# Seams of a two-layer diffusion step: the first two chunks' high parts made by ScalarE straight from the transposes

## The reference: what is computed

```python
def layer(x, mod, p, ...):
    sh1, sc1, g1, sh2, sc2, g2 = jnp.split(mod, N_MOD, axis=-1)
    h = rms_norm(x, p["g_pre_mix"]) * (1.0 + sc1) + sh1
    y, ckv, krope, hf, hb = mixer(h, p, ...)      # projections, attention, RG-LRU, w_out
    x = x + g1 * rms_norm(y, p["g_post_mix"])
    h = rms_norm(x, p["g_pre_ffn"]) * (1.0 + sc2) + sh2
    x = x + g2 * rms_norm(swiglu(h, p), p["g_post_ffn"])
    return x, ckv, krope, hf, hb
```

## Time and profile before

| | before |
|---|---|
| device time, median of 3 runs (lowest to highest) | 1274.1 us (1274.09 to 1274.28) |
| span of the profiled execution | 1276.9 us |
| PE busy | 1239.6 us, 97% |
| PEld, DVE, ACT busy | 1145.4, 853.3, 658.0 us |
| POOL busy | 19.6 us |
| the three seams, time of tile 0's last root | 375.9, 664.3, 992.4 us |

### The profile page before, as it was taken

How to read it: one execution, slowest core, us unless ns; L and a number is a source line. 1 busy time by engine, 2 the same in 40 slices (tenths; PEclk the granted TensorE clock), 3 DMA queues, 4 the chain that set the end, 5 groups by cost and what they waited for, 6 DMA issues and landing times.

```text
span 1276.9 us, 19343 instructions
## 1 busy us (share of the span) xinstructions
PE 1239.6 (97%) x7345; PEld 1145.4 (90%) x7345; DVE 853.3 (67%) x1391; ACT 658.0 (52%) x1161; POOL 19.6 (2%) x41
## 2 busy tenths in 40 slices
PE   6999999999999999999999999999999999999998
PEld 4899989978879999998879999998898899999886
DVE  2697684764869888868858885856566748433423
ACT  5479874754464333332255999647446533333322
POOL 0000000200000000000000000011000000000000
PEclk9999999999989999999999999999999999999999
DMA  9645555332437776758815333442224347444441
GB/s 336 211 116 178 182 165 197 103 120 100 124 117 221 255 224 203 235 178 272 286 49 144 110 100 115 128 140 75 76 80 152 107 146 231 132 132 132 158 165 49
DMA packets 131103, 199.33 MB, mean 156 GB/s; under 512 B 10330, under 2 KB 70980, under 8 KB 131012
## 3 DMA queue, kind: packets, MB, share of 16 engines
q1 hardware_dynamic: 131012, 198.11, 48.8%
HBM read 196.16 MB, written 1.92 MB: 155 GB/s over the span
## 4 chain that ended last, share of the span: by engine, by line
PE 77%; DVE 11%; ACT 6%; issue 2%; DMA 2%; SPq 1%; DVEq 0%; ACTq 0%
PE bank L755 16%; PE bank L762 16%; PE bank L763 16%; PE bank L885 5%; PE bank L887 5%; PE bank L886 5%; DVE weight_low L1700 3%; ACT weight_high L1318 2%; PE bank L1185 1%; DVE lru_h L1998 1%; PE bank L1209 1%; ACT sq L1326 1%; DVE lru_tau L2002 1%; DVE lru_i L1994 1%; PE bank L1194 1%
## 5 line engine op out<-in xcount | busy, mean ns | idle before, releaser
L762 PE MATMUL bank<-act_low,weight_high 128*128 128x384 f32 x1440 | 488.5, 339 | 3.7 <-DVE weight_low L1700 3.6
L763 PE MATMUL bank<-act_high,weight_low 128*128 128x384 f32 x1440 | 483.4, 336 | 0.0
L1700 DVE TENSOR_TENSOR weight_low<-raw,weight_high 128x1024 fp32r<-128x1024 f32 (+5 forms) x282 | 320.2, 1153 | 169.0 <-ACT weight_high L1318 168.6
L1318 ACT ACTIVATE weight_high<-raw 128x1024 fp32r<-128x1024 f32 (+5 forms) x282 | 273.2, 995 | 232.9 <-DMA raw<-in_w_ffn_in 79.7
L755 PE MATMUL bank<-act_high,weight_high 128*128 128x384 f32 x1440 | 314.9, 339 | 4.6 <-ACT sq L1409 2.8
L762 PEld LDWEIGHTS bank<-act_low,weight_high 128*128 128x128 f32 x1440 | 271.8, 189 | 10.9 <-DVE weight_low L1700 5.8
L763 PEld LDWEIGHTS bank<-act_high,weight_low 128*128 128x128 f32 x1440 | 271.8, 189 | 0.0
L755 PEld LDWEIGHTS bank<-act_high,weight_high 128*128 128x128 f32 x1440 | 253.7, 188 | 11.8 <-issue 3.7
L885 PE MATMUL bank<-weight_high,hid_high 128*128 128x512 f32 x264 | 103.2, 391 | 0.0
L886 PE MATMUL bank<-weight_low,hid_high 128*128 128x512 f32 x264 | 102.8, 389 | 0.0
L887 PE MATMUL bank<-weight_high,hid_low 128*128 128x512 f32 x264 | 102.8, 389 | 0.0
(11 more groups left out here) (268 smaller groups left out, 1486.5 us busy)
## 6 DMA issues: line engine op xcount, KB each, us to landing
raw<-in_w_ffn_in SPq DMA_DIRECT2D x176, 256.0 KB, 4.2
mod_weight<-in_w_mod SPq DMA_DIRECT2D x80, 512.0 KB, 4.7
raw<-in_w_in SPq DMA_DIRECT2D x72, 512.0 KB, 3.8
raw<-in_w_ffn_out SPq DMA_DIRECT2D x44, 512.0 KB, 4.7
first_mod<-in_w_mod SPq DMA_DIRECT2D x4, 2048.0 KB, 13.8
raw<-in_w_o_lru SPq DMA_DIRECT2D x16, 512.0 KB, 3.7
raw<-in_w_out SPq DMA_DIRECT2D x16, 512.0 KB, 3.7
raw<-in_w_o_mla SPq DMA_DIRECT2D x8, 512.0 KB, 3.9
```

The source lines that it names most:

```text
L762: nc.tensor.matmul(o, view[0][:, kk, cols], low[:, k, :], start=False, stop=False)
L763: ins = nc.tensor.matmul(o, view[1][:, kk, cols], high[:, k, :], start=False, stop=k == total - 1)
L1318: nc.scalar.activation(high, w, ACT.Copy).then_inc(*AC.step())
L1700: nc.vector.tensor_tensor(low, w, high.bitcast(F), ALU.subtract).then_inc(*VE.step())
```

## The change

- **High parts of chunks 0 and 1.** They are no longer copies of `t`. ScalarE applies scale and shift itself, reading the transposes from the PSUM bank (`high_of`): first the sample tokens of both chunks (step `sample_high`), then the prompt tokens (step `hh`). VectorE still computes `t` for the low part, in `seam_shifts`.
- **Low parts of chunks 0 and 1** are made in two pieces each (256 and 128 tokens) in place of one of 384.
- **Scaling of tile 0** is cut 256 + 768 channels in place of 512 + 512. The long piece comes after chunk 0's low part.
- **Transposes.** Of tile 0 only chunks 0 and 1 are transposed ahead of the first product; each waits for `sample_high` of its chunk. Chunks 2, 3, 4, 5, 6, 7 come at positions 0, 1, 3, 5, 11, 15 of the first job. From chunk 4 on, `turn_next` waits for `hh` of the bank's earlier chunk as well as for `hfull`.
- **Unread transposes:** six new ones behind the first two of tile 1, and sixteen in place of eight further on.
- **Weight splits:** ScalarE's split of the third weight tile is moved ahead of `hh` of chunk 2; VectorE's split of the second one stands behind both chunks' low parts.

```diff
-                    pe.wait_ge(*at(VE, "scaled", pre, a, c // 4))
+                    pe.wait_ge(*at(VE, "scaled", pre, a, c // 4 if a > 0 else min(c // 2, 1)))
...
                         turned(atp, pre, job, c, (1,), "turn_first", layer=lp)
+                    for c in (0, 1, 0, 1, 0, 1):
+                        nc.tensor.transpose(turn_bank(job, c)[:, P:2 * P], ytok[:, 1, P * c:P * c + P], ident[:, :])
...
                     for a in (1, 2):
-                        for c in (2, 3, 2, 3):
+                        for c in (2, 3, 2, 3, 2, 3, 2, 3):
                             nc.tensor.transpose(turn_bank(job, c)[:, P * a:P * a + P], ytok[:, a, P * c:P * c + P], ident[:, :])
-                    for c in range(4):
-                        if c < 2:
-                            pe.wait_ge(*atp(VE, "sample", pre, c))
+                    for c in range(2):
+                        pe.wait_ge(*atp(AC, "sample_high", pre, c))
                         turned(atp, pre, job, c, (0,), "turned", layer=lp)
-                    turn_next(lp, pre, job, 4)
...
-                    pe.wait_ge(*atp(VE, "hfull", pre, c - (4 if c < 6 else 2)))
-                    turned(atp, pre, job, c, TILES, "turned", layer=lp)
+                    if c >= 4:
+                        pe.wait_ge(*atp(VE, "hfull", pre, c - (4 if c < 6 else 2)))
+                        pe.wait_ge(*atp(AC, "hh", pre, c - (4 if c < 6 else 2)))
+                    turned(atp, pre, job, c, TILES if c >= 4 else (0,), "turned", layer=lp)
...
-                              between=turn_between(l, "ffn", "wo", {3: (5,), 11: (6,), 15: (7,)}) if j == 0 else None,
+                              between=turn_between(l, "ffn", "wo", {0: (2,), 1: (3,), 3: (4,), 5: (5,), 11: (6,), 15: (7,)}) if j == 0 else None,
...
                     if pre is not None:
+                        atp = in_layer(lp)
+                        dst_scale, shift, ready = {"ffn": (scale2, 3, "scale2"), "mix": (scale1, 0, "scale1")}[pre]
+                        ac.wait_ge(*at(VE, ready))
+                        for c in (0, 1):
+                            ac.wait_ge(*atp(VE, "sample", pre, c))
+                            high_of(turn_bank(job, c), dst_scale, shift, pre, lp, c, 1, "sample_high", pre, c)
+                        for c in (0, 1):
+                            ac.wait_ge(*atp(PE, "turned", pre, c))
+                            high_of(turn_bank(job, c), dst_scale, shift, pre, lp, c, 0, "hh", pre, c)
                         highs(next_job, 1, layer=lp)
-                        act_highs(pre, lp, next_job, {1: 2, 4: 3})
+                        highs(next_job, 2, layer=lp)
+                        act_highs(pre, lp, next_job, {4: 3}, range(2, C))
...
+                def seam_shifts(pre, lp, job, next_job, dst_scale, shift):
...
+                    for c in (0, 1):
+                        ve.wait_ge(*atp(PE, "turn_sample", pre, c))
+                        shifted(pre, lp, job, dst_scale, shift, c, 1)
+                        VE.also("sample", pre, c, layer=lp)
+                    scaled(pre, lp, 0, (0,))
+                    for c in (0, 1):
+                        ve.wait_ge(*atp(AC, "sample_high", pre, c))
+                        ve.wait_ge(*atp(VE, "sample", pre, c))
+                        low(c, 1)
+                        ve.wait_ge(*atp(AC, "hh", pre, c))
+                        shifted(pre, lp, job, dst_scale, shift, c, 0)
+                        VE.also("hfull", pre, c, layer=lp)
+                        own()
+                        low(c, 0, "h", pre, c)
+                        if c == 0:
+                            scaled(pre, lp, 0, (1,))
+                    lows(next_job, 1, layer=lp)
+                    normalise(pre, lp, job, next_job, dst_scale, shift, {3: 2, 5: 3}, range(2, C))
```

More of the change, by code:

```diff
@@ L1014, in _ @@
                 else:
[L1015 removed]
+                    split_job("lx0", hh, hl, ready=(VE, "h", "mix"), ready_high=(AC, "hh", "mix"), between=turn_between(l, "mix", "fo", {0: (2,), 1: (3,), 3: (4,), 5: (5,), 11: (6,), 15: (7,)}))
                 split_job("lx1", hh, hl)
@@ L1394, in seam, with high_of, act_highs @@
                     if pre is not None:
-                        highs(next_job, 1, layer=lp)
-                        act_highs(pre, lp, next_job, {1: 2, 4: 3})
-                def act_highs(pre, lp, next_job, after):
+                        atp = in_layer(lp)
[7 more added lines that the diff above has]
+                            high_of(turn_bank(job, c), dst_scale, shift, pre, lp, c, 0, "hh", pre, c)
+                        highs(next_job, 1, layer=lp)
+                        highs(next_job, 2, layer=lp)
+                        act_highs(pre, lp, next_job, {4: 3}, range(2, C))
+                def high_of(src, dst_scale, shift, pre, lp, c, g, *label):
+                    toks = GROUPS[g][1]
+                    nc.scalar.activation(hh[:, c, toks], src[:, toks], ACT.Identity, scale=dst_scale[:, c, g:g + 1],
+                                         bias=mod[:, shift * C + c, g:g + 1]).then_inc(*AC.step(*label, layer=lp))
+                def act_highs(pre, lp, next_job, after, chunks=range(C)):
                     atp = in_layer(lp)
-                    for c in range(C):
+                    for c in chunks:
                         ac.wait_ge(*atp(VE, "hfull", pre, c))
@@ L1829, in shifted, with normalise @@
                                             mod[:, shift * C + c, g:g + 1], ALU.mult, ALU.add).then_inc(*VE.step())
-                def normalise(pre, lp, job, next_job, dst_scale, shift, after, chunks=range(C), early=()):
+                def normalise(pre, lp, job, next_job, dst_scale, shift, after, chunks=range(C)):
                     atp = in_layer(lp)
@@ L1841, in normalise @@
                     own()
[L1842 to L1847, removed]
                     for c in chunks:
@@ L1852, in normalise @@
                         for g in range(2):
-                            if g == 0 or c not in early:
-                                shifted(pre, lp, job, dst_scale, shift, c, g)
+                            shifted(pre, lp, job, dst_scale, shift, c, g)
                         VE.also("hfull", pre, c, layer=lp)
@@ L1860, in normalise, with low, scaled @@
                     low(chunks[-1])
-                def scaled(pre, lp, a):
+                def seam_shifts(pre, lp, job, next_job, dst_scale, shift):
+                    atp = in_layer(lp)
+                    def low(c, g, *label):
+                        toks = GROUPS[g][1]
+                        nc.vector.tensor_tensor(hl[:, c, toks], t[c % 2][:, toks], hh[:, c, toks].bitcast(F), ALU.subtract
+                                                ).then_inc(*VE.step(*label, layer=lp))
+                    own()
[11 more added lines that the diff above has]
+                        VE.also("hfull", pre, c, layer=lp)
+                        own()
+                        low(c, 0, "h", pre, c)
[3 more added lines that the diff above has]
+                    normalise(pre, lp, job, next_job, dst_scale, shift, {3: 2, 5: 3}, range(2, C))
+                def scaled(pre, lp, a, parts=(0, 1)):
                     ve.wait_ge(*in_layer(lp)(AC, "x_root", pre, a))
                     own()
-                    for h in range(2):
-                        half = slice(512 * h, 512 * h + 512)
+                    for h in parts:
+                        half = slice(512 * h, 512 * h + 512) if a > 0 else (slice(0, 256), slice(256, D))[h]
                         nc.vector.tensor_scalar(ytok[:, a, half], x[:, a, half], ss[:, 21 + a:22 + a], None, ALU.mult
```

4 lines of the change are left out of this document (2 added, 2 removed).

## The result

| | before | changed |
|---|---|---|
| median of 17 runs each | 1274.82 us | 1277.77 us |
| lowest to highest | 1272.64 to 1277.34 | 1276.91 to 1279.25 |
| ratio, 95% interval | | 1.0022 [1.0015, 1.0029] |
| span of the profiled execution | 1276.9 | 1276.5 |

The account below looks back on a forecast made before the run. PE was taken to bound the kernel, with VectorE and ScalarE setting each seam at chunk 6, R + 10.20. Seam changes of +0.1, +1.4 and -0.2 us on 1274.1 gave 1275.4 us; the 8 in 10 range was 1272.1 to 1277.8.

Parts of the forecast that it names:

- The chain of a seam: Seam from last root activation R: first product 0.55 us earlier, 0.37 us stall at chunk 2, chunk 6's transposes at R + 10.20.
- The named cause: Chunk 6's transposes: PE stands 1.07 us, for VectorE's shift of chunk 4, 0.81 later, and for ScalarE's copy of it.
- The first rival: At chunk 6: VectorE quicker by 1 us or more, no wait, PE's work sets R + 9.13; 1272.2 us, chance 0.17.
- The second: Two seams: clock falls anyway, unread transposes delay tile 0, chunk 6 near R + 11.15; 1277.3 us, chance 0.13.
- The sum: Three seams against the profiled execution: +0.1, +1.4 and -0.2, together +1.3 us, carried over to the median: 1275.4 us.
- third rival: All seams: earlier runs never lost the clock, so each seam loses 1.4 us; +4.1, 1278.2 us, chance 0.10.
- the stated range: Whole kernel: the 8 in 10 range, 1272.1 to 1277.8 us, from the first rival to between the second and third.
- the forecast's own range: Whole kernel: unknown costs move the three seams' sum by -1.2 to +1.8 us, giving 1274.2 to 1277.2 us.
- the three classes: Whole kernel, against a bound of 0.2% or 2.5 us: faster 0.09, same 0.65, slower 0.26.
- The clock: All three seams: fourteen more unread transposes keep PE's upper clock; a fall had cost 1.29 and 1.53 us a seam.

Follow-up runs that it names:

- the two fastest versions: Changed kernel with all its lateness taken out, with the added unread transposes (1272.83 us, ratio 0.9986) and with the old number of them (1274.22 us, 0.9996).
- The version that pays: Changed kernel with whole scaling first, chunks 2 and 3 transposed early, high-part wait for chunks 4 and 5 only, later VectorE weight splits: 1272.83 us, ratio 0.9986.

## Why the prediction was right, and where its size was off

**The chain of a seam: right.** Predicted for a clean seam: first product R + 1.6, stall ahead of chunk 2's transpose 0.4, shift of chunk 4 to R + 9.49, its copy to R + 10.05, chunk 6 at R + 10.20. Measured: R + 1.48, chunk 2's transpose 0.22 later than it would follow without a wait, released by `scaled` as forecast (the view puts only 0.05 of it down as idle), shift to R + 9.51, copy to R + 10.06, chunk 6 at R + 10.15. The first product was better than forecast mainly because PE's first transpose started 0.09 us behind the end of the first sample high (374.35 to 374.44), where the sum had taken 0.15. That gains nothing, as nothing did in the forecast: PE waits later anyway. The prices that no row of before showed came out as taken: 0.55 and 0.46 us for the highs (0.57 and 0.46), 0.62 for 768 channels (0.62), 0.42 and 0.29 for the low parts.

**The named cause: right.** Take out either half of it and the predicted share comes back: the copy 0.6 us a seam (forecast 0.56), VectorE's order 1.0 by later splits. The two don't add up, since the copy costs nothing once VectorE is early. The edit "wait alone, in the kernel before" puts 0.54 of the 1.36 us of a clean seam into a kernel that has nothing else of the change. The first rival (chunk 6 does not wait) is refuted by the wait itself. The second (unread transposes in the way) needed a fall before the sixteen are over. That did not occur in any of the 21 seams that have them; at the upper clock the sixteen take 1.91 us and PE then stands for 0.78 to 0.92. What they would cost after an earlier fall stays untested.

**The step that failed in size: how many seams of before run at the lower clock.** The sum charged the change against the one profiled execution, with two fallen seams of three, and said that the difference carries over to the median. A fallen seam of before is as long as a clean one of the changed kernel (23.29 and 23.56 against 23.38), so each seam counted as fallen took 1.3 to 1.5 us off the loss. In the later profiles of kernels with the old number of unread transposes, five seams of twelve fell. With two falls of three the sum gives +1.3; with none it is three times 1.36, +4.1; with 1.25 falls, about +2.3, beside a measured +2.95 (the ratio's interval is 1.9 to 3.7 us). The 1.25 rests on twelve seams of four kernels, and the falls outside the seams are in none of these sums. The text had the end of this scale as its third rival, with a hint of the direction in hand: the profiled execution was well above the median. I gave it 0.10, with the argument that nothing in the program differs, and used the profiled execution as typical; the kernel before, run again, fell in one seam in place of two. Of the 2.4 us between forecast (1275.4) and result, 0.7 is the base, 1274.1 from three runs where 17 gave 1274.82. The other 1.65 is the size of the change, and this step explains about 1.0 of it; the rest is inside the interval and has no cause shown. That the measured 1277.77 lies in the stated range is in part luck: it is 0.03 us below the upper bound and above the forecast's own range, which ended at 1277.2. Of the three classes the one with 0.26 came out, just over its bound of 0.2%, with an interval on both sides of that bound.

**The clock: wrong in one seam.** I expected the fourteen transposes to keep it in all seams and named a PEclk of 0.5 in a seam as a sign of being wrong. That sign came, in the second seam of the changed kernel, where the fall cost 0.45 us. Over all profiles they kept it in most seams, not in all: of the seven profiles with them two seams of 21 fell (the changed kernel's second, the third of one experiment); of the five with the old number, the first profile of before among them, seven of fifteen did. The Trainium skill's "TensorE: Matmul & The Clock Gate", Part 4 (PE-mode transpose), says that transposes don't count as busy for the gate as products do. These counts speak against it as a plain rule, since stretches of transposes alone kept the upper clock (6.50 us in the earlier trace rows). They leave room for it as a warning, since sixteen of them ahead of a seam's first products did not save the changed kernel's second seam. What the added transposes are worth in time is not shown: the two fastest versions differ by 1.4 us, by medians from two chips whose ratios overlap, and in the kernel before they gave no clear difference. In the changed kernel itself they could bring almost nothing, since its wait at chunk 6 hides most of a fall.

**Why the idea did not pay as built.** PE was idle while it waited for tile 0's high part. The change shortened that idle time by 0.65 us and moved five transposes out of it into product time, where they cost about as much (0.59 by the forecast). Even with no wait at all this leaves PE where it was, as the experiment with the whole scaling shows: R + 8.64 for R + 8.66 at the last product ahead of chunk 6. The version that pays keeps chunks 2 and 3 in the idle time as well: its seam ends at R + 21.80 for R + 22.02.

## What to carry to other kernels

When a critical step is shortened, list what stood in its shadow: work moved out of an idle stretch costs its full length, and the next buffer that comes free late takes the rest. A wait added for safety should name the engine that really reads the buffer; on the bank's later users it cost 0.54 us a seam, though ScalarE reads `t` there and not the bank. And where the clock falls in some executions and not in others, price a change against seams at the same clock, and learn from several executions how often each kind occurs, before the sum is made.

## What was not expected of the hardware

- The same program loses the clock in different seams from one execution to the next: the kernel before in its first and third seam in one profile, in its first alone in another. Its runs spread over 4.7 us (1272.64 to 1277.34), the changed kernel's, in which a seam's fall costs 0.45 us, over 2.3.
- The same stretch far from any seam goes both ways too: behind 1.18 us in which PE stood still, at about 42 us, the granted clock was 0.50 in seven of twelve profiles and 1.00 in five.
- The profile's releaser can be an instruction of the wrong engine: where PE waited for VectorE and ScalarE and ScalarE's copy came last, it named VectorE's low part, for which PE does not wait and which ended 0.19 us before PE started (383.86 and 384.05).
